# Exchanging rotary halves by transfers between partitions instead of a rotation product, for the later queries and keys

## What is computed

```python
q, k, v, xbc, z, dt_raw = jnp.split(h @ w_in, IN_SPLITS, axis=-1)
def apply_rope(t, cos, sin):          # heads of 64 features
    t1, t2 = jnp.split(t, 2, axis=-1)
    rot = jnp.concatenate([-t2, t1], axis=-1)
    return t * cos + rot * sin
q = apply_rope(q, cos, sin) * 64 ** -0.5
k = apply_rope(k, cos, sin)
```

## Time and profile before

| | |
|---|---|
| median of 3 runs | 2279.61 us (2276.6 to 2281.89) |
| span of the profiled execution | 2278.5 us |
| PE busy | 2238.8 us (98%) |
| DVE, ACT, POOL busy | 1698.9, 917.6, 230.4 us |
| queue of SP's transfers, share of the 16 DMA engines | 20.0% |

### The profile page before, as it was taken

The page is one execution under the profiler, slowest core; times in us unless marked ns, Lnnn a source line. Parts: engine busy times, 40 slices in busy tenths (PEclk is TensorE's granted clock), DMA queues, the critical chain, the costliest instruction groups (busy, mean ns, idle before and its releaser), DMA issues. The chain is left out here.

```text
span 2278.5 us, 29774 instructions
## 1 busy us (share of the span) xinstructions
PE 2238.8 (98%) x10460; PEld 1835.5 (81%) x10460; DVE 1698.9 (75%) x2547; ACT 917.6 (40%) x1614; POOL 230.4 (10%) x213
## 2 busy tenths in 40 slices
PE   9999999999999999999999999999999999999998
PEld 7888888888877877778788777788888888888887
DVE  8877777777759787786666686879877777777767
ACT  6322222222334576777531774225332222222224
POOL 0000000000000344443100226100000000000000
PEclk9999999999999999999999999999999999999999
DMA  4111111111323001101221135133121111111123
GB/s 161 56 51 47 50 55 55 55 50 38 124 100 114 20 10 38 38 10 56 75 67 54 65 121 175 56 121 111 38 70 50 47 55 55 55 55 52 41 87 135
DMA packets 54748, 154.65 MB, mean 68 GB/s; under 512 B 6144, under 2 KB 8192, under 8 KB 52608
## 3 DMA queue, kind: packets, MB, share of 16 engines
q1 hardware_dynamic: 54656, 153.46, 20.0%
HBM read 132.14 MB, written 21.30 MB: 67 GB/s over the span
## 5 line engine op out<-in xcount | busy, mean ns | idle before, releaser
L1094 DVE TENSOR_TENSOR acc<-psum,acc 128x512 f32<-128x512 f32 x288 | 197.8, 690 | 161.0 <-PE psum L583 158.2
L710 ACT CAST t_hi<-t_raw 128x512 fp32r<-128x512 f32 x144 | 89.6, 622 | 319.9 <-DVE t_raw L900 303.0
L583 PE MATMUL psum<-act_hi,tile_lo 128*128 128x512 f32 x544 | 211.9, 389 | 0.0
L582 PE MATMUL psum<-act_lo,tile_hi 128*128 128x512 f32 x544 | 211.9, 389 | 0.0
L581 PE MATMUL psum<-act_hi,tile_hi 128*128 128x512 f32 x544 | 211.9, 389 | 0.0
L732 ACT ACTIVATE sum<-sum 128x512 f32<-128x512 f32 x72 | 45.6, 633 | 245.1 <-DVE sum L1048 150.4
L2097 PE MATMUL psum<-norm_hi,tile_hi 128*128 128x512 f32 x320 | 129.2, 404 | 1.8 <-DVE z_scaled L2505 1.8
L2414 DVE TENSOR_TENSOR probs_t_lo<-psum,probs_t_hi 128x512 fp32r<-128x512 f32 x144 | 97.1, 685 | 39.2 <-ACT probs_t_hi L2331 38.3
L2099 PE MATMUL psum<-norm_hi,tile_lo 128*128 128x512 f32 x320 | 125.1, 391 | 0.0
L2098 PE MATMUL psum<-norm_lo,tile_hi 128*128 128x512 f32 x320 | 125.0, 391 | 0.0
L581 PEld LDWEIGHTS psum<-act_hi,tile_hi 128*128 128x128 f32 x544 | 102.2, 188 | 21.2
(11 more groups left out here) (436 smaller groups left out, 5870.2 us busy)
## 6 DMA issues: line engine op xcount, KB each, us to landing
tile_lo_raw<-in_d SPq DMA_DIRECT2D x40, 512.0 KB, 4.3
gate_raw<-in_gu SPq DMA_DIRECT2D x36, 512.0 KB, 3.8
up_raw<-in_gu SPq DMA_DIRECT2D x72, 256.0 KB, 3.7
raw_tile<-in_w_att SPq DMA_DIRECT2D x28, 512.0 KB, 3.7
x_scratch<-acc SPq DMA_DIRECT2D x32, 256.0 KB, 2.1
cum_rows<-cum_scratch SPq DMA_DIRECT2D x8, 1024.0 KB, 4.7
raw_tile<-in_w_out SPq DMA_DIRECT2D x15, 512.0 KB, 3.6
gate_up_lo_raw<-in_gu SPq DMA_DIRECT2D x7, 1024.0 KB, 6.1
```

The costliest lines, as they stand in the source:

```text
L582: pe.matmul(o, w_h[:, s, d, :], a_l[:, s, x], start=False, stop=False)
L583: mm = pe.matmul(o, w_l[:, s, d, :], a_h[:, s, x], start=False, stop=(s == 1))
L710: act.copy(to, of).then_inc(sem(p + "_t_hi"), 1)
L1094: v.tensor_tensor(x, banks(4 + d % 4), x, ALU.add).then_inc(sem(p + "_acc"), 1)
```

## The change

It replaces the rotation product of the seven later tiles (14 halves). A new buffer `q_swapped` (128x512) is filled from `q_raw` by four transfers of 32 partitions each, issued by SP (`swap_sp`), that exchange the row blocks 0 with 1 and 2 with 3. The sign that the matrix carried goes into the sine table: ACT forms a third quarter table with the negated sine, SP writes it out too, and the sine table is read from the negated and the plain one in turn. DVE's sine product reads `q_swapped` in place of bank 7. The first three tiles keep the product, with a matrix without sign. Bank 7 is free for the next half as soon as DVE has read it. There is one buffer for the exchange: a swap waits for the sum of the half before it. The planner is given a cost of 4.0 for a swap and a line of its own for the sine steps, and orders everything anew.

```diff
@@ tables @@
             act.activation(cosq[:], ang[:], ACT.Sin, scale=0.5).then_inc(sem("rope_sin"), 1)
+            act.activation(turns[:], ang[:], ACT.Sin, scale=-1.0).then_inc(sem("rope_sin"), 1)
             act.activation(sinq[:], ang[:], ACT.Sin).then_inc(sem("rope_sin"), 1)
...
-            for n, t in enumerate((cosq, sinq)):
+            for n, t in enumerate((cosq, sinq, turns)):
...
-            for n, t in enumerate((cos, sin)):
+            for t, table in ((cos, (0, 0, 0, 0)), (sin, (2, 1, 2, 1))):
                 for r in range(4):
                     sp.dma_start(t[32 * r:32 * r + 32, :].rearrange("f (q t) -> f q t", q=4),
-                                 rope[n].rearrange("q f t -> f q t")).then_inc(sem("rope_in"), 16)
+                                 rope[table[r]].rearrange("q f t -> f q t")).then_inc(sem("rope_in"), 16)
@@ planner @@
-                        add("DVE", "pieces", ("evict", f, h), 0.69, last[f], row[h])
+                        add("DVE", "pieces", ("evict", f, h), 0.69, last[f], *row[h])
...
-                        add("PE", "fill", ("rot", f, h), 0.78, taken[f, 1], ("evict", f, h), taken[f, 0])
-                        add("DVE", "pieces", ("sin", f, h), 1.4, ("rot", f, h), ("cos", f, h))
-                        taken[f, 1] = row[h] = ("sin", f, h)
+                        add("SP", "swap", ("swap", f, h), 4.0, ("evict", f, h), swapped)
+                        add("DVE", "sin", ("sin", f, h), 1.4, ("swap", f, h), ("cos", f, h))
+                        row[h], swapped = [("swap", f, h), ("cos", f, h)], ("sin", f, h)
@@ steps @@
-                mm = pe.matmul(banks(7), rot[:], qr[:, x], start=True, stop=True)
...
+        def sin_dve(v, w, h):
+            t, x = TILES[w][1], half(h)
+            v.wait_ge(sem("q_swap"), 64 * (swaps(w, h) + 1))
+            v.wait_ge(sem("at_cos"), 2 * w + h + 1)
+            v.tensor_tensor(qro[:], qro[:], sin[:, x], ALU.mult).then_inc(sem("at_sin"), 1)
+            v.wait_ge(sem("at_sin"), swaps(w, h) + 1)
+            v.tensor_tensor(qn[:, t, x], qn[:, t, x], qro[:], ALU.add).then_inc(sem("at_sum"), 1)
+
+        def swap_sp(sp, w, h):
+            sp.wait_ge(sem("pj_read"), pieces(w, h) + 1)
+            sp.wait_ge(sem("at_sum"), 2 * w + h)
+            for r in range(4):
+                sp.dma_start(qro[32 * r:32 * r + 32, :], qr[32 * (r ^ 1):32 * (r ^ 1) + 32, half(h)]).then_inc(sem("q_swap"), 16)
```

More of the change, by code:

```diff
@@ L2051, in mixer_plan @@
             rank = dict(TAIL_RANK)
-            rank |= {("PE", "score"): 1, ("PE", "turn"): 2, ("PE", "values"): 3, ("PE", "fill"): 9, ("DVE", "pieces"): 1,
+            rank |= {("PE", "score"): 1, ("PE", "turn"): 2, ("PE", "values"): 3, ("PE", "fill"): 9, ("DVE", "pieces"): 1, ("DVE", "sin"): 1,
                     ("DVE", "weights"): 8, ("ACT", "weights"): 8, ("DVE", "conv"): 7, ("ACT", "qk"): 6, ("DVE", "qk"): 6}
@@ L2063, in probs, with pieces, swaps, piece_pe @@
             return (pe1 if i % 2 else pe0)[:, hh, :]
[L2065 to L2073, removed]
-                mm = pe.matmul(banks(7), rot[:], qr[:, x], start=True, stop=True)
[L2075 to L2083, removed]
+        FIRST_PIECES = 12
+        def pieces(w, h):
+            return FIRST_PIECES + 2 * (w - 3) + h
+        def swaps(w, h):
+            return 2 * (w - 3) + h
+        def piece_pe(pe, w, h, part):
+            x = half(h)
+            if part == 0:
+                pe.wait_ge(sem("pj_read"), pieces(w, h))
+                pe.wait_ge(sem("at_w_lo"), w + 1)
+            for k in range(part * KT // PARTS, (part + 1) * KT // PARTS):
+                pe.matmul(banks(7), wh[:, w % 2, k, :], nh[:, k, x], start=(k == 0), stop=False)
+                pe.matmul(banks(7), wh[:, w % 2, k, :], nl[:, k, x], start=False, stop=False)
+                mm = pe.matmul(banks(7), wl[:, w % 2, k, :], nh[:, k, x], start=False, stop=(k == KT - 1))
+            if part == PARTS - 1:
+                mm.then_inc(sem("pj_mm"), 1)
         def tile_pe(pe, f, h, part):
@@ L2381, in unit_end_pool, with piece_dve @@
             gp.tensor_tensor(x, x, ovt[:], ALU.add).then_inc(sem("at_ov_add"), 1)
[L2383 to L2393, removed]
-            else:
-                wait(v, "at_sum", m)
-                v.scalar_tensor_tensor(out=qr[:, x], in0=banks(bank), scalar=0.125 if t < 2 else 1.0,
-                                       in1=rb[:, x], op0=ALU.mult, op1=ALU.mult).then_inc(sem("pj_read"), 1)
+        def piece_dve(v, w, h):
+            t, x = TILES[w][1], half(h)
+            v.wait_ge(sem("pj_mm"), pieces(w, h) + 1)
+            if w > 3:
+                v.wait_ge(sem("q_swap"), 64 * (swaps(w - 1, h) + 1))
+                v.wait_ge(sem("at_cos"), 2 * (w - 1) + h + 1)
+            else:
+                v.wait_ge(sem("at_sum"), 6)
+            v.scalar_tensor_tensor(out=qr[:, x], in0=banks(7), scalar=0.125 if t < 2 else 1.0,
+                                   in1=rb[:, x], op0=ALU.mult, op1=ALU.mult).then_inc(sem("pj_read"), 1)
+        def sin_dve(v, w, h):
+            t, x = TILES[w][1], half(h)
+            v.wait_ge(sem("q_swap"), 64 * (swaps(w, h) + 1))
[8 more added lines that the diff above has]
+                sp.dma_start(qro[32 * r:32 * r + 32, :], qr[32 * (r ^ 1):32 * (r ^ 1) + 32, half(h)]).then_inc(sem("q_swap"), 16)
         def att_dve(v):
@@ L2954, in _ @@
                       .then_inc(sem("att_out"), 16)
+                elif step == "swap":
+                    swap_sp(sp, e[0] + 3, e[1])
                 elif step == "w_in":
```

44 lines of the change are left out of this document (18 added, 26 removed).

## The result

The changed kernel took **2287.70 us** (median of 5 runs, 2285.11 to 2291.69) against 2277.49 us of the kernel before on the same chip (5 runs, 2276.60 to 2281.89). The ratio is 1.0033 with a 95% interval of 1.0020 to 1.0047: **slower**, by 0.2 to 0.5%. The forecast was 2276.4 us, the range ended at 2287.

The account below looks back on a forecast made before the run. PE was taken as the bound, with small waits in attention where fill lacks. The terms -12.0 + 0.3 - 7 + 8.5 + 7.0 = -3.2 us gave 2276.4 us against a median of 2279.61, range 2266 to 2287.

Parts of the forecast that it names:

- Rotations off PE: In attention, 14 rotation products of 0.86 us each leave PE: 12.0 us less.
- Sine product: On DVE, the 14 sine products read both operands from SBUF instead of one from PSUM: +0.3 us.
- Swaps: In attention, a swap takes 3.4 us, under the planner's 4.0, so no instruction waits for it: cost 0.
- rival D: At attention's group changes, scores wait for the last key and query tile; 12.0 us given back, 2279.6 us; chance 0.07.
- rival B: In attention, DVE waits for swaps of 5.5 us, 21 us lost, half reaching PE: +10.5, 2286.9 us; chance 0.14.
- Bank 7 free earlier: In attention, fill can run where bank 7 was held until the second sine product: -7 us, twice the lower bound.
- the two thin places: Group 3's units 2 to 5 and group 1's units 5 and 6, where the new order has almost no fill.
- what was called certain: In attention, the waits on the sine product that certainly go, 1.9 + 1.7 = 3.6 us.
- Fill runs out: PE idles where fill is lacking: +8.5 us in group 3's units 2 to 5, +7.0 in group 1's units 5 and 6.
- Rival A: Attention's chain is shorter without fill than taken, both fill-poor places near their lower bounds: -12.2, 2267.4 us; chance 0.22.
- rival C: Both fill-poor places of attention cost their upper bounds, only the certain waits recovered: +5.9, 2285.5 us; chance 0.11.
- Behind attention: The stages after attention are not touched by the change: no cost or gain.

Follow-up runs that it names:

- e1: The changed kernel in its own order, without the 56 transfers and the waits on them (rotary values not computed): 2281.28 us, ratio 1.0006 to the kernel before.
- e2: The changed kernel with the planner's swap cost 5.0 in place of 4.0, ordered anew: 2281.44 us, ratio 1.0007 to the kernel before.
- e11: The kernel before, 14 rotations and no swap, with the tile order and bank edit of e9: 2279.39 us, ratio 0.9993 to the kernel before.
- e9: The changed kernel with swap cost 5.0, bank 7 for both halves of the first two x tiles, early z tiles between q tiles: 2265.83 us, ratio 0.9930.
- e5: The kernel before in its own order, its 14 rotation products cut from 512 to 8 columns: 2284.55 us, ratio 1.0025 to the kernel before.
- e3: The changed kernel with both halves of the first two x tiles in bank 7, ordered anew: 2282.43 us, ratio 1.0013 to the kernel before.

## Why the prediction was wrong

The sum had -3.2 us and attention of the profiled run came out at +8.6. Three steps failed: the swaps that were to cost nothing cost 3.3 us of this difference (about 6 us in the timed runs of e1 and e2), the earlier bank gave about half of its 7 us (3.3 of the difference), and the granted clock had no term (5.1, an estimate). That the swaps cost time is shown by experiment; the other two are read from traces.

*Rotations off PE, 12.0 us.* The size holds: 9.3 us of PE's records less, 14 us (give or take 4) between e11 and e9. Entered in full it held only with its condition, other work in its place. PE is busy 98%, but most units with rotations are nearly as long as DVE's work, and rows 8 said so: unit 6 of group 1 had DVE busy 16.95 of 19.1 us. In e5, where nothing moved in, those seven units did not get shorter. The 12 us could only be had as room for fill, and the prediction gave that one term, the last.

*No term for the granted clock.* It was missing altogether. By the mean clock over the runs, (1 - clock) x time went from 8.1 to 14.6 us, +6.5 us. In the profiled run, the fastest of the five, two stretches of attention show it (3.4 us of the 18.1 at 0.81, 1.7 of the 20 at 0.91). e5 isolates it best. That it falls after PE has idled is what the rows show; no run held PE's work equal and changed only the clock, so its share of the time stays an estimate.

*Sine product, +0.3.* Right within half a us: 692 ns at the median, 1031 at the longest, 10.3 us for the 14 where they took 9.5.

*Swaps, cost 0.* This step failed. A transfer lands in 2.0 us at the median, as taken (1.9), but SP issues one every 0.63 us, not every 0.49, and at worst 1.7. So a swap takes 3.9 us at the median and up to 4.9, where 3.4 was forecast and the planner has 4.0. That left DVE no margin: three of the six swaps that it waited for took no more than 4.04 us themselves. Five of the six stood right behind the sum of the half before, since there is one buffer; the prediction had that chain in rival D and not here. e1 and e2 both put the waits at 6 us of time. That is rival B's mechanism in small: 7.4 us of DVE's time where it had 21, 6 us of time where it had 10.5. B came nearest, 2286.9 us, with a chance of 0.14, and in part by luck, since it kept the -7.

*Bank 7 free earlier, -7.* The sign was right and the size was not, and in the changed kernel the gain is hidden. Take the time of the 26 units outside the two thin places, less 0.68 us for each part of fill and 0.86 for each rotation in them. It rose by 1.8 us. In e1, which has the same order without transfers and a full clock in these units, it fell by 3.4 (an estimate from the trace). So the bank gave about what was called certain, 3.6. The 5.0 us between the two kernels in these units are 1.7 us of lowered clock at the end of group 0 and 3.3 of swaps. (The two thin places took 2.4 us longer in e1, with 5.1 us more of lowered clock in them.) The bank is not free at the last matmul either, only when DVE has read it: that wait grew from 2.5 to 5.1 us.

*Fill runs out, +8.5 and +7.0.* Right within 2 us each: the four units took 41.8 us (40.0 taken), the two 30.9 (29.4), which is +10.3 and +8.5. The second holds 3.4 us of lowered clock, about what both are above their forecast. e3 shows that the shortage is real. Rival A fell with it (over 38 us), rival C had the size of these places and the wrong reason for the rest. Rival D didn't happen: the scores of a new group waited 1.1 us in all for their queries.

*Behind attention, nothing.* The last value product ends 27.7 us later than before, with 28 more parts of fill (19.0 us) ahead of it, which is +8.6 us at attention's end: -12.0, +10.3, +8.5 and the 1.8 of the other units. The profiled runs differ by 4.6 in all. Most of the 4.0 between lies in a later stretch (before, then the changed kernel):

```profile
1410.00:1620.00 210.00, 208.35 (x955) 171.59 (x954) 170.78 (x230) 74.69 (x101) 22.43 (x9) 0.96 0.28 96
```

```profile
1410.00:1620.00 210.00, 209.09 (x974) 172.31 (x972) 170.94 (x228) 79.20 (x105) 30.15 (x12) 0.98 0.29 100
```

The clock fell there in both kernels, by 0.02 less in this one run of the changed kernel, up to 4 us of the 210. Whether the change has a part in that is open.

## What to carry to other kernels

Price work taken off the busiest engine by the stretch in which it stands: if another engine is busy for nearly all of that stretch, its removal opens a gap and shortens next to nothing, until other work is moved into the gap, and the order has to be made for that. Give the new steps what they take from the first instruction to the last, issue included, at their worst and not at their median, and look for a single buffer that ties one of them to the one before (e2). Put work that doesn't need them in between (e9). Before taking PE work away, read the granted clock beside it and count the gap that you open as a possible loss too.

## What the runs showed of the hardware

- Stretches at 1.2 GHz, in which 512 columns take 0.43 us in place of 0.23, came in the changed kernel and in e5 beside or a few us behind a gap of 1.0 to 2.5 us on PE (2.46 us in the changed kernel, 1.64 at the first in e5). With the fourteen products of 0.86 us beside such gaps the clock stayed full in attention, though the longest gap there was 1.47 us; with 8 columns of each left it fell at six places, and up to 10 us of 2285 went that way. A gap is not enough by itself: e9 has 20 waits for low parts, of up to 2.6 us, and one stretch of attention below full clock (0.83 from 850 to 860 us).
- A transfer of 64 KB from SBUF to SBUF over 32 partitions lands 2.0 us after its issue at the median (1.9 to 3.1), about as long as a store of 256 KB to memory (2.1) and longer than one of 64 KB (1.5).
- SP's issue of such a transfer is 0.59 us at the median, 0.51 to 1.68, where the issue seen at the start of the kernel was 0.45; four of them (2.4 us) are over half of the swap's 3.9 us.
